# Five raw weight buffers and five ring slots instead of three and six, with a new deal of the low parts, in a two-block transformer kernel

## The chip, the cores and the metric

The kernel runs on one core of one Trainium2 chip. The metric is the device time of one execution in microseconds (us); smaller is better. All activations stay on the chip; the weights, 364 pieces of 512 KB, stream from HBM while TensorE (PE) works.

## The reference, cut to what matters

Batch 1, 256 tokens (T), model width 1024. The first block has two hybrid layers, the second one layer:

```python
for layer in range(2):                                  # hybrid_layer
    p = split_columns(rmsnorm(x, norm_g) @ w_in)        # 19 groups of columns
    qk = silu(causal_dwconv(concat(p.ml_q, p.ml_k)))    # 4 taps
    y_ml  = norm(mlstm(...) * sigmoid(ml_o)) * silu(ml_z)
    y_gla = norm(gla(...)) * silu(gla_r)
    y_dsa = attention(top-64 keys by index score, + rel_bias[bucket(j - i)]) * silu(dsa_z)
    x = x + concat(y_ml, y_gla, y_dsa) @ w_out
h = x + 0.5 * swiglu(norm(x), ffn1)                     # 1024 -> 2816 -> 1024
n = norm(h)
attn  = causal attention, 8 heads of 64
zg    = gelu(...);  gm = zg_u * (W_s @ layernorm(zg_v) + b_s)   # spatial gating
gates = sigmoid(n @ w_gate + b_gate)
h = h + (gates_a * (attn @ wa) + gates_b * (gm @ wb)) @ w_out
h = h + 0.5 * swiglu(norm(h), ffn2)
out = norm(h)
```

Everything is float32.

## The kernel before

**Tiling.** Activations lie transposed: 128 channels on the partitions, 256 tokens along the free dimension. A weight piece ("slot") is 128 x 1024, eight tiles of 128 x 128. Each layer uses 90 slots (74 for `w_in`, 16 for `w_out`), each FFN 66, the mixer 20 + 16 + 8 + 8. A product is done in three matmuls per weight tile: weight and activation are both split into a part rounded to float32r ("high") and the rest ("low"), and high x high, low x high and high x low are summed in PSUM. So a slot is 24 matmuls of 256 columns (or 12 of 512). `xs` holds both parts of the normed input, `ys` those of the input to an output projection.

**The weight pipeline.** SyncE (SP) loads slot g into `raw[g % 3]` as soon as `lo[g % 3]` says that the low part of slot g-3 was made. ScalarE (ACT) copies it, rounded, to `ring[g % 6]` high (`split`, line 392) after PE has used slot g-6 (`slots_used`). VectorE (DVE, line 854, one instruction of 1024 columns) makes the low part of every third slot, GpSimd (POOL, line 291, two halves) that of the others. PE waits on `lo` before it uses a slot. On ACT, DVE and POOL `split(p)` stands in a written-out order between the other work of position p and converts slot p + RING.

**The stages.** In front of each layer, FFN and mixer, PE begins on the input before the norm's factor is known (`first_two`, `early`, line 409), because the factor can be multiplied to the results afterwards (`early_result`, line 892). Squares of `x` are summed (lines 398, 871, 1496), ACT forms the root (`factor`, lines 373 to 380, with a table load), DVE refines it (883 to 887), the normed input is written to PSUM (`normed`, 898) and split again into `xs` (`norm` on ACT, line 424, `norm_lo` on DVE, line 910), and the later products read that. `norm` stands behind the first few `split`s in ACT's order. In a layer PE's first small matmuls after that (line 1641, index logits) wait for DVE's and ACT's gate work (`gate_softplus` 497, `gate_scan` 965 to 974) and `early_result(5)`. From slot 12 to 26 come the small products of gated linear attention (eight levels, lines 1067 to 1097, 1693), from 26 the convolution (`convolve`, line 1154, whose PSUM bank PE waits for), then gates (491, 1207 to 1211), then `w_out` (`sum_slot`, line 1557).

**At the start** one matmul forms the relative bias rows (4 x 384), ACT copies them (line 434) and issues one DMA (line 438) that writes each row 128 times to DRAM (`bias_rows`, 4 x 128 x 384).

**FFN.** Per tile f of 128 hidden channels three slots: gate, up (line 1509), and the down slot of tile f-2 (1557). DVE does lines 1288, 1293, 1298, 1302 and the low part 916, ACT the tanh (683) and the high part (688).

**Mixer.** In `spatial` PE does line 1933 after the layer norm (DVE line 1405), DVE adds the bias and multiplies (1413, 1414). ACT's `branch_hi` (773) and DVE's `branch_lo` (1418) split the eight branch inputs, four of them at the last gate slot; the branch products (line 1509, 12 matmuls each) wait for four low parts at a time.

## Time and profile before

| what | value |
|---|---|
| median of 3 runs | 1270.58 us (1267.05 to 1275.13) |
| the profiled execution | 1263.89 us, span of its instructions 1262.0 us |
| mean granted TensorE clock | 0.974 of 2.4 GHz |
| busy: PE, DVE, ACT, POOL | 1173.5, 823.0, 655.4, 698.7 us |
| weights and other data moved | 199.66 MB, mean 158 GB/s |

The profiled execution lies 1.89 us above its span and 6.69 us below the median. A group's row gives its busy time, the mean of one instruction, and the idle time of the engine ahead of it with what ended it. A PE that waits inside a run of matmuls can be shown busy, since ends of matmuls are modelled; counts of matmuls in a stretch tell more than its busy time.

### The profile page before, as it was taken

The page shows a single profiled execution, that of the slowest core. Times are in us where ns is not written, and L with a number is a line of the kernel's source. Part 1 is how long each engine was busy: PE and PEld are TensorE (multiplying, and loading weights), DVE is VectorE, ACT ScalarE, POOL GpSimd, SP SyncE. Part 2 cuts the span into 40 slices and gives each one's busy share as a digit, 9 for nine tenths or more (in the row PEclk, how much of TensorE's full clock was granted, in tenths as well). Part 3 has the DMA queues.
Part 4 walks back from the last instruction along what each step waited for, and adds up shares of the span by engine and source line. Part 5 has one row for each costly group of instructions (what it writes and reads, how often), then busy time and mean ns, then how long its engine had stood idle before and what let it go on. Part 6 is the DMA issues. An engine that isn't in the chain of part 4 may idle for free.

```text
span 1262.0 us, 25299 instructions
## 1 busy us (share of the span) xinstructions
PE 1173.5 (93%) x9214; PEld 1111.7 (88%) x9214; DVE 823.0 (65%) x1301; ACT 655.4 (52%) x1020; POOL 698.7 (55%) x530
## 2 busy tenths in 40 slices
PE   5499998999998989999999999999899889999996
PEld 4488798899997969989999999998878889999996
DVE  4366979486667598866676645555656756655664
ACT  3464485346456637644655544444657435544442
POOL 2243547555655355664566576667565555666662
PEclk9698999999998999999999999999999989999999
DMA  6343334544554433354456455555453445566561
GB/s 208 94 137 122 125 115 150 168 157 163 177 163 149 135 123 105 134 185 143 162 180 204 157 197 189 198 193 185 149 174 127 141 144 175 167 200 200 187 196 50
DMA packets 57715, 199.66 MB, mean 158 GB/s; under 512 B 6388, under 2 KB 9492, under 8 KB 57620
## 3 DMA queue, kind: packets, MB, share of 16 engines
q1 hardware_dynamic: 53856, 193.90, 46.6%
q10 hardware_dynamic: 3764, 4.47, 1.5%
q8 instruction: 62, 1.02, 0.3%
q14 instruction: 33, 0.27, 0.1%
HBM read 196.52 MB, written 1.84 MB: 157 GB/s over the span
## 4 chain that ended last, share of the span: by engine, by line
PE 29%; POOL 28%; issue 23%; DVE 11%; DMA 5%; ACT 3%; POOLq 0%; DVEq 0%; ACTq 0%; SPq 0%
POOL ring L291 26%; PE ps L1509 18%; PE ps L1557 6%; DMA raw<-in_w 5%; PE ps L1547 2%; DVE ring L854 2%; ACT ring L392 1%; DVE gs L1067 1%; PE ps L1660 1%; POOL dec L305 1%; DVE gat L1097 0%; ACT xs L424 0%; DVE xs L1418 0%; DVE xs L864 0%; POOL dec L306 0%
## 5 line engine op out<-in xcount | busy, mean ns | idle before, releaser
L291 POOL TENSOR_TENSOR ring<-raw,ring 128x512 fp32r<-128x512 f32 x484 | 666.8, 1401 | 510.2 <-ACT ring L392 508.8
L1509 PE MATMUL ps<-xs,ring 128*128 128x256 f32 x5424 | 666.7, 283 | 32.9 <-DVE mq L892 15.9
L1509 PEld LDWEIGHTS ps<-xs,ring 128*128 128x128 f32 x5424 | 647.4, 192 | 45.2 <-issue 17.5
L392 ACT ACTIVATE ring<-raw 128x1024 fp32r<-128x1024 f32 x364 | 382.5, 1055 | 251.6 <-DMA raw<-in_w 197.2
L854 DVE TENSOR_TENSOR ring<-raw,ring 128x1024 fp32r<-128x1024 f32 x122 | 179.0, 1467 | 156.6 <-ACT ring L392 154.6
L1557 PE MATMUL ps<-ys,ring 128*128 128x256 f32 x2016 | 240.2, 278 | 4.1 <-DVE ys L916 2.9
L1557 PEld LDWEIGHTS ps<-ys,ring 128*128 128x128 f32 x2016 | 235.8, 188 | 4.8 <-issue 3.5
L1547 PE MATMUL ps<-ring,xs 128*128 128x512 f32 x480 | 120.6, 404 | 6.4 <-DVE xs L910 3.2
L1547 PEld LDWEIGHTS ps<-ring,xs 128*128 128x128 f32 x480 | 88.9, 190 | 28.0 <-issue 9.1
L1154 DVE SCALAR_TENSOR_TENSOR ca<-ps,par,ca 128x253 f32<-128x253 f32 (+2 forms) x96 | 45.1, 477 | 11.4 <-ACT ca L476 10.0
L916 DVE TENSOR_TENSOR ys<-ca,ys 128x256 fp32r<-128x256 f32 x44 | 42.2, 960 | 13.8 <-ACT ys L688 13.8
L683 ACT ACTIVATE ex<-ex 128x256 f32<-128x256 f32 x44 | 18.1, 415 | 61.2 <-DVE ex L1288 61.2
L491 ACT ACTIVATE ex<-ps 128x256 f32<-128x256 f32 x48 | 18.3, 382 | 53.6 <-PE ps L1509 53.5
L916 DVE TENSOR_TENSOR ys<-y,ys 128x256 fp32r<-128x256 f32 x32 | 30.0, 938 | 23.2 <-ACT ys L619 23.1
L1519 PEld LDWEIGHTS ps<-xs,ring 128*128 128x128 f32 x240 | 31.0, 204 | 10.8 <-issue 8.7
L1519 PE MATMUL ps<-xs,ring 128*128 128x256 f32 x240 | 31.9, 297 | 8.8 <-ACT xs L409 5.7
L688 ACT ACTIVATE ys<-ca 128x256 fp32r<-128x256 f32 x44 | 18.2, 413 | 39.4 <-DVE ca L1302 39.3
L1293 DVE SCALAR_TENSOR_TENSOR ca<-ps,rms 128x256 f32<-128x256 f32 x44 | 18.3, 417 | 29.0 <-PE ps L1509 29.0
L1302 DVE SCALAR_TENSOR_TENSOR ca<-ex,ca 128x256 f32<-128x256 f32 x44 | 32.4, 737 | 1.5
L1298 DVE TENSOR_TENSOR ca<-ca,ex 128x256 f32<-128x256 f32 x44 | 30.8, 700 | 1.4
L476 ACT ACTIVATE ca<-ps,par 128x256 f32<-128x256 f32 x32 | 17.8, 557 | 25.4 <-DVE mq L1169 13.8
L538 ACT ACTIVATE gs<-gs 128x256 f32<-128x256 f32 x16 | 6.8, 423 | 45.7 <-DVE gs L1067 45.7
(256 smaller groups left out, 1053.9 us busy)
## 6 DMA issues: line engine op xcount, KB each, us to landing
raw<-in_w SPq DMA_DIRECT2D x364, 512.0 KB, 3.5
y<-bias_rows ACTq DMA_DIRECT2D x6, 256.0 KB, 3.2
x<-in_x SPq DMA_DIRECT2D x4, 256.0 KB, 7.1
out_y<-y SPq DMA_DIRECT2D x4, 256.0 KB, 2.2
const<-in_const SPq DMA_DIRECT2D x1, 896.0 KB, 10.7
bias_rows<-lg ACTq DMA_DIRECT2D x1, 768.0 KB
par<-in_par ACTq DMA_DIRECT2D x3, 181.0 KB, 2.4
dec<-in_wT ACTq DMA_DIRECT2D x1, 512.0 KB, 4.7
```

The costliest lines, as they stand in the source:

```text
L291: last = pool.tensor_tensor(ring[:, g % RING, 1, half], raw[:, g % RAW, half], ring[:, g % RING, 0, half].bitcast(F32), ALU.subtract)
L392: act.activation(ring[:, g % RING, 0, :], raw[:, g % RAW, :], ACT.Copy).then_inc(S["hi"], 1)
L491: ins = act.activation(ex[:, m % 4, :], src[:, 0:T], ACT.Tanh, scale=0.5)
L854: tt(ring[:, g % RING, 1, :], raw[:, g % RAW, :], ring[:, g % RING, 0, :].bitcast(F32), ALU.subtract).then_inc(lo[g % RAW], 1)
L916: tt(ys[:, at, 1, :], src, ys[:, at, 0, :].bitcast(F32), ALU.subtract).then_inc(S["y_lo"], 1)
L1154: ins = stt(dst[:, late:T], bank[:, 0:T - late], w[:, j:j + 1], dst[:, late:T], ALU.mult, ALU.add)
L1298: step(tt(ca[:, f % 2, :], ca[:, f % 2, :], ex[:, 2 + f % 2, :], ALU.mult))
L1302: stt(ca[:, f % 2, :], ex[:, f % 2, :], 1.0, ca[:, f % 2, :], ALU.add, ALU.mult)\
L1509: last = mm(ps[bank][:, half * T:(half + 1) * T], ring[:, slot % RING, wp, (at + k) * P:(at + k + 1) * P], rhs(k, xp), start=(i == 0), sto ...
L1519: return mm(ps[bank][:, 0:T], ring[:, slot % RING, wp, k * P:(k + 1) * P], rhs(k, xp), start=start, stop=stop)
L1547: last = mm(ps[banks[tt]][:, :], xs[:, 2 * q + k, xp, tt * P:(tt + 1) * P], ring[:, slot % RING, wp, k * 512:(k + 1) * 512], start=(q == 0 ...
L1557: ins = mm(ps[4 + n // 2][:, n % 2 * T:(n % 2 + 1) * T], ring[:, slot % RING, wp, n * P:(n + 1) * P], ys[:, at, xp, :], start=(first and n ...
```

## The change

Five edits, made together:

1. `RAW` 3 to 5 and `RING` 6 to 5. A raw buffer and a ring slot now have the same index, and each load waits for the low part of the slot five before.
2. Who makes a low part is told by the stage (`on_vector`): in a layer positions 3 and 6, then every fourth up to 42, then every third; in an FFN every second, in the mixer every third. POOL makes the others.
3. The relative bias is formed on all 128 partitions by four matmuls (one head each), copied by four activations of 128 x 384, and stored by one DMA whose source is those 128 partitions.
4. The spatial product stays in PSUM, its jobs on PE and DVE come one slot later, and the first branch products wait for each part by itself instead of four.
5. The FFN loops are unrolled on all engines, SP's loops too. Besides: at the start the loads of `x` and slot 1 are interleaved and `par` is asked for after `rb` and `hot`; in a layer `row_results` and `gate_softplus` come earlier in ACT's order, and two explicit table loads are dropped.

```diff
-RAW = 3
-RING = 6
+RAW = 5
+RING = 5
+def on_vector(p):
+
+    if p < 0:
+        return p in (-RING, -RING + 3)
+    if p < LAYER_SLOTS:
+        if p < EARLY + 2:
+            return p in (3, 6)
+        return p % 4 == 2 if p < 42 else p % 3 == 0
+    if FFN1_AT <= p < MIX_AT or p >= FFN2_AT:
+        f = p - FFN1_AT if p < MIX_AT else p - FFN2_AT
+        return f % 2 == 1 and f < FFN_SLOTS - 4
+    return p % 3 == 0
...
-            sp.dma_start(raw[:, 0, :], d["w"][0]).then_inc(slot_in[0], 16)
-            for c in range(N_UPDATES):
+            fetch(0, 0)
+            for c in range(2):
                 sp.dma_start(x[:, 2 * c:2 * c + 2, :], d["x"][:, 2 * c:2 * c + 2, :]).then_inc(x_in[c], 16)
...
+            fetch(1, 1)
+            for c in range(2, N_UPDATES):
+                sp.dma_start(x[:, 2 * c:2 * c + 2, :], d["x"][:, 2 * c:2 * c + 2, :]).then_inc(x_in[c], 16)
+            for g in range(2, RAW):
+                fetch(g, g)
...
+            for g in range(RAW, TOTAL_SLOTS):
+                sp.wait_ge(lo[g % RAW], g // RAW)
+                fetch(g, stored_at(g))
...
-            act.wait_ge(S["bias_ps"], 1)
-            act.activation(bias_row, ps[5][0:4, 0:HOT], ACT.Copy).then_inc(S["bias_sb"], 1)
+            for h in range(4):
+                act.wait_ge(S["bias_ps"], h + 1)
+                act.activation(relu4[:, h, :], ps[4 + h][:, 0:HOT], ACT.Copy).then_inc(S["bias_sb"], 1)
             split(-RING + 3)
             squares(0)
-            act.wait_ge(S["bias_sb"], 1)
-            act.dma_start(bias_rows.ap(), bias_row.rearrange("h (o n) -> h o n", o=1).broadcast_to((4, P, HOT)))\
-                .then_inc(S["bias_out"], 16)
+            act.wait_ge(S["bias_sb"], 4)
+            act.dma_start(bias_rows.ap().rearrange("h p n -> p h n"), relu4).then_inc(S["bias_out"], 16)
...
                 def gate_softplus():
-                    log_and_exp()
...
                 split(1, it, LAYER_SLOTS)
+                row_results()
                 split(2, it, LAYER_SLOTS)
-                row_results()
                 split(3, it, LAYER_SLOTS)
                 norm(it, gains, V_G, it * LAYER_SLOTS + EARLY)
+                gate_softplus()
                 split(4, it, LAYER_SLOTS)
                 split(5, it, LAYER_SLOTS)
-                gate_softplus()
...
                 g = p + RING
-                if g % RAW == 0:
+                if on_vector(p):
                     dve.wait_ge(S["hi"], reg * per + (g + 1))
...
-                dst = ca[:, pr % 2, :]
+                dst = ps[4 + pr][:, T:2 * T]
                 step(tt(dst.rearrange("p (c i) -> p c i", c=2), src, b, ALU.add))
-                stt(y[:, pr, :], y[:, pr, :], 0.5, dst, ALU.mult, ALU.mult).then_inc(S["sg_done"], 1)
+                stt(dst, y[:, pr, :], 0.5, dst, ALU.mult, ALU.mult).then_inc(S["sg_done"], 1)
...
-                     29: [(spatial, 0), (spatial, 1)], 31: [(spatial, 2), (spatial, 3)]}
+                     30: [(spatial, 0), (spatial, 1)], 32: [(spatial, 2), (spatial, 3)]}
...
-            mm(ps[5][0:4, 0:HOT], rb[:, :], hot, start=True, stop=True).then_inc(S["bias_ps"], 1)
+            for h in range(4):
+                mm(ps[4 + h][:, 0:HOT], rb[:, h:h + 1].broadcast_to((32, P)), hot,
+                   start=True, stop=True).then_inc(S["bias_ps"], 1)
...
-            jobs2[29] = [(spatial, 0), (spatial, 1)]
-            jobs2[31] = [(spatial, 2), (spatial, 3)]
+            jobs2[30] = [(spatial, 0), (spatial, 1)]
+            jobs2[32] = [(spatial, 2), (spatial, 3)]
...
-                    if n == 0:
-                        pe.wait_ge(S["b_lo"], 4 * g + 4)
-                    last = tile_product(n % 4, g, slot, lambda k, part: branch(4 * g + k, part), range(4), at=4 * g)
+                    last = tile_product(n % 4, g, slot, lambda k, part: branch(4 * g + k, part), range(4), at=4 * g,
+                                        ready=(lambda k, part: pe.wait_ge(
+                                            S["b_lo" if part else "b_hi"], 4 * g + k + 1)) if n == 0 else None)
```

## Rows read from the trace of the kernel before

**Rows 1.** The waits, all engines and then PE's: who waited for whom, us, times, longest.
```profile
ACT ring L392 <- DMA raw<-in_w: 197.2, 127, 15.9
...
PE ps L1693 <- DVE gat L1095: 4.7, 2, 2.3
```

**Rows 2.** FFN1 and FFN2: us, busy (xmatmuls), other engines' busy, PEclk, DMA share, GB/s.
```profile
713.00:880.00 167.00, 166.81 (x1421) 166.25 (x1421) 88.96 (x120) 77.98 (x101) 115.11 (x81) 1.00 0.57 192
...
1082.00:1246.00 164.00, 164.00 (x1450) 164.00 (x1449) 99.41 (x124) 75.31 (x100) 102.59 (x76) 1.00 0.56 180
```

**Rows 3.** The timeline of the first 71 us: start, duration, instruction, idle before.
```profile
16.24 1.24 ACTq L438 DMA_DIRECT2D bias_rows<-lg  x1
...
21.79 1.13 PE L1496 MATMUL ps<-y,const 128*128 128x256 f32 x4 [0.72 <-DVE y L871]
...
36.25 1.06 ACT L392 ACTIVATE ring<-raw 128x1024 fp32r<-128x1024 f32 x1 [15.93 <-DMA raw<-in_w]
...
39.85 1.28 ACT L373 ACT_TABLE_LOAD   x1
...
43.83 0.42 DVE L892 SCALAR_TENSOR_TENSOR mq<-ps,rms 104x256 f32<-104x256 f32 x1
...
53.71 1.06 ACT L392 ACTIVATE ring<-raw 128x1024 fp32r<-128x1024 f32 x1 [10.79 <-DMA raw<-in_w]
...
70.39 0.49 PE L1641 MATMUL ps<-ik,mq 64*128 64x128 f32 x4 [1.66 <-ACTq L457]
```

**Rows 4.** DMA from 14 to 58 us: busy share in tenths, GB/s, ACT's queue.
```profile
DMA  6067485267527722222222225932222267682100
GB/s 252 37 164 306 63 222 164 22 68 239 138 22 156 250 24 22 22 52 69 70 79 77 68 71 91 293 68 22 22 25 25 22 149 264 192 354 115 52 7 0
...
q10 hardware_dynamic: 516, 0.79, 15.0%
```

**Rows 5.** The timeline of the same place in layer 1.
```profile
378.56 0.42 DVE L892 SCALAR_TENSOR_TENSOR mq<-ps,rms 104x256 f32<-104x256 f32 x1
...
387.15 1.06 ACT L392 ACTIVATE ring<-raw 128x1024 fp32r<-128x1024 f32 x1 [3.13 <-DMA raw<-in_w]
...
388.72 11.04 PE L1509 MATMUL ps<-xs,ring 128*128 128x256 f32 x72 [3.71 <-ACT xs L424]
...
395.23 1.10 DVE L965 SCALAR_TENSOR_TENSOR gat<-gat 4x256 f32<-4x256 f32 x1 [1.24 <-ACT gat L498]
...
400.98 0.49 PE L1641 MATMUL ps<-ik,mq 64*128 64x128 f32 x4 [1.22 <-ACTq L457]
```

**Rows 6.** Busy time of a short stretch; PEclk is the third number from the end.
```profile
388.00:400.00 12.00, 11.04 (x72) 10.87 (x72) 9.68 (x15) 7.14 (x14) 6.96 (x4) 0.76 0.36 125
```

**Rows 7.** The timeline of FFN1 at 789 us, and of FFN2 at 1104.
```profile
789.85 5.82 PE L1509 MATMUL ps<-xs,ring 128*128 128x256 f32 x48
...
1104.42 5.60 PE L1509 MATMUL ps<-xs,ring 128*128 128x256 f32 x48
```

**Rows 8.** The timeline of the mixer, from its entry to its branch products.
```profile
883.46 5.89 PE L1519 MATMUL ps<-xs,ring 128*128 128x256 f32 x48 [2.99 <-ACT xs L409]
...
904.46 1.06 ACT L392 ACTIVATE ring<-raw 128x1024 fp32r<-128x1024 f32 x1 [5.39 <-DMA raw<-in_w]
...
909.59 3.23 DVE L910 SCALAR_TENSOR_TENSOR xs<-ps,gains,xs 128x256 fp32r<-128x256 f32 x8 [1.81 <-ACT xs L424]
910.61 2.99 PE L1547 MATMUL ps<-ring,xs 128*128 128x512 f32 x12 [3.22 <-DVE xs L910]
...
993.92 1.44 PE L1933 MATMUL ps<-dec,gv 128*64 128x128 f32 x16 [3.23 <-DVE gv L1405]
...
1013.54 5.55 DVE L1418 TENSOR_TENSOR xs<-y,xs 128x256 fp32r<-128x256 f32 x4 [1.80 <-ACT xs L773]
...
1019.14 2.93 PE L1509 MATMUL ps<-xs,ring 128*128 128x256 f32 x12 [3.32 <-DVE xs L1418]
```

**Rows 9.** DVE's groups in FFN1, 720 to 880 us: busy, mean ns, idle before.
```profile
L854 DVE TENSOR_TENSOR ring<-raw,ring 128x1024 fp32r<-128x1024 f32 x19 | 29.5, 1550 | 58.6 <-ACT ring L392 58.6
```

More of the change, by code:

```diff
@@ L45 @@
 IN_SLOTS, OUT_SLOTS = 74, 16
+EARLY, M_EARLY = 6, 8
 LAYER_SLOTS = IN_SLOTS + OUT_SLOTS
@@ L286, in split @@
                 g = p + RING
-                if g % RAW:
+                if not on_vector(p):
                     pool.wait_ge(S["hi"], reg * per + (g + 1))
@@ L333, in ffn @@
             def ffn(at):
-                for p in range(4):
-                    split(at + p)
-                loops = (FFN_TILES - 2) // 4 - (1 if at == FFN2_AT else 0)
-                with pool.Fori(0, loops) as i:
-                    for p in range(12):
-                        split(at + 4 + p, i, 12)
-                for p in range(at + 4 + 12 * loops, at + FFN_SLOTS):
+                for p in range(at, at + FFN_SLOTS):
                     if p + RING < TOTAL_SLOTS:
@@ L712, in ffn @@
                 split(at + 3)
-                loops = (FFN_TILES - 2) // 4 - (1 if last else 0)
-                with act.Fori(0, loops) as i:
-                    four(i, 2)
-                if last:
-                    four(0, 2 + 4 * loops)
-                else:
+                for f in range(2, FFN_TILES):
+                    tile(f)
+                if not last:
                     act.wait_ge(S["par2_in"], 16)
@@ L772, in branch_hi @@
                     act.wait_ge(S["xs_free"], (LAYERS + 1) * (KT - 1) + k - 3)
-                act.activation(branch(k, 0), y[:, (k + 4) % 8, :], ACT.Copy).then_inc(S["b_hi"], 1)
+                act.activation(branch(k, 0), branch_in(k), ACT.Copy).then_inc(S["b_hi"], 1)
             def layer_root():
@@ L1248, in _ @@
                     normed(it, c)
-                split(0, it, LAYER_SLOTS)
                 for r in range(2, 4):
@@ L1253, in _ @@
                 gate_abs()
-                split(3, it, LAYER_SLOTS)
+                for p in range(EARLY):
+                    split(p, it, LAYER_SLOTS)
                 early_result(4)
@@ L1284, in ffn, with gate, up @@
             def ffn(at, n, h_done, y_done, last):
[L1286 to L1287 removed]
+                def gate(f, slot):
+                    dve.wait_ge(S["slots_used"], slot + 1)
                     stt(ex[:, 2 + f % 2, :], ps[2 * (f % 2)][:, 0:T], -0.5, rms[:, 0:T], ALU.mult, ALU.mult)\
                         .then_inc(S["ffn_t"], 1)
[L1291 to L1292 removed]
+                def up(f, slot):
+                    dve.wait_ge(S["slots_used"], slot + 1)
@@ L1312, in four @@
-                def four(i, f0):
-                    step.restart()
-                    for f in range(f0, f0 + 4):
-                        p = at + 4 + 3 * (f - 2)
-                        gate(f, p, i)
-                        next_split(p, i)
-                        up(f, p + 1, i)
-                        up_gate(f, i)
-                        product(f, i)
-                        next_split(p + 1, i)
-                        product_lo(f, i)
-                        next_split(p + 2, i)
+                        split(p)
@@ L1325, in ffn, with tile @@
+                def tile(f):
+                    p = at + 4 + 3 * (f - 2)
+                    gate(f, p)
+                    next_split(p)
+                    up(f, p + 1)
+                    up_gate(f)
+                    product(f)
+                    next_split(p + 1)
+                    product_lo(f)
+                    next_split(p + 2)
                 factor(n)
@@ L1334, in ffn @@
                     split(p)
-                loops = (FFN_TILES - 2) // 4 - (1 if last else 0)
-                with dve.Fori(0, loops) as i:
-                    four(i, 2)
-                if last:
-                    four(0, 2 + 4 * loops)
+                for f in range(2, FFN_TILES):
+                    tile(f)
                 update_x(n, at + FFN_SLOTS, 0.25)
@@ L1440, in _ @@
                 normed(LAYERS, c)
-            split(MIX_AT)
-            split(MIX_AT + 3)
+            for p in range(MIX_AT, MIX_AT + 5):
+                split(p)
             for r in range(4, 7):
@@ L1445, in _ @@
             norm_lo(LAYERS, gains2, U_MIX)
-            split(MIX_AT + 6)
+            for p in range(MIX_AT + 5, MIX_AT + M_EARLY):
+                split(p)
             early_result(7)
```

126 lines of the change are left out of this document (50 added, 76 removed).

## The prediction

> **What bounds the kernel now.** I read the busy times first (PE is the fullest, 1173.5 of 1262.0 us in the table), then counted matmuls per stretch, since a PE that waits can look busy. 364 slots of 24 matmuls (value slots: 12 of double width) are 8736 units. In FFN2 PE does 1450 matmuls in 164 us, 0.1131 us each, so one slot costs 2.71 us and the weights alone 988 us [rows 2]. The other 274 us are the smaller products, half-rate clock, and waits. So any stretch in which PE runs at the FFN2 rate cannot gain, and the question is where it does not.
>
> Then the waits. ACT waited 197.2 us in 127 waits for weights, the longest 15.9 us [rows 1]: a raw buffer is reloaded only after its low part is made. Most of that costs PE nothing; what matters is where ACT's next job is on PE's path. The timeline shows three kinds of places. At the start, ACT stands 15.93 us and later 10.79 us at a load, and the norm's factor and the second split of the input are queued behind those [rows 3]. At the norm of layer 1 it stands 3.13 us, at that of the mixer 5.39 us [rows 5, 8]. In FFN1 PE is slower than in FFN2: 1421 matmuls in 167 us, 0.1175 us each, at the same granted clock of 1.00 [rows 2]; 48 matmuls take 5.82 us instead of 5.60 [rows 7]. I call the two the slow and the fast step of PE. I found the slow step to begin after short waits of PE in several places, and it stays for a long time after supply has recovered; this is an observation of order, not a shown cause.
>
> **The change part by part**, against the profiled execution (1263.89 us).
>
> *Start.* The DMA issued at 16.24 us has 512 packets of 1.5 KB. For long stretches after it the DMA engines together are 0.2 to 0.3 busy and move 22 to 79 GB/s, ahead of it and after it up to 354 [rows 4]: that is a few of the 16 engines, full, while each weight load needs its share of these few too. Its queue has 516 packets in 15.0% of 16 engines over 44 us, 105.6 engine-us, 0.205 us a packet [rows 4]. The new source has 128 partitions, so I expect all 16 engines with 32 packets each: 6.6 us at this price, and no load waits longer than that. The Trainium skill, page "DMA: Bandwidth & Descriptors", section "Why a DMA increments its semaphore by 16 and not by 1", says that the slowest dimension of both access patterns sets the number of engines, 4 before and 16 after; the trace agrees by its share of about 4/16.
>
> After the change slots 0 to 4 are asked for at once. Their 2.5 MB, x and the constants are about what is moved before 20 us now, so slot 5 should land by about 23 us. PE is through the first two results about when it starts on the squares, 21.79 us [rows 3]; the four copies of 128 x 384 cost ACT some 1.5 us more there. ACT then does one split (1.06), and from its table load (39.85) to the first scaled result (43.83) are 3.98 us [rows 3]: 23 + 1.06 + 3.98 = 28. From that instruction to PE's line 1641 layer 1 takes 400.98 - 378.56 = 22.4 us [rows 5], and 6 less after the next item: 28 + 16.4 = 44.4, against 70.39 [rows 3]. That is 26; for the copies and for `par`, asked for later, I take 1 off: **25**. Bounds: 6 if loads still stall as before, 29.
>
> *Norm of layer 1.* The load wait of 3.13 us ahead of slot 99 goes, since with five buffers its buffer is free five slots earlier. `norm` starts about 3.5 us earlier, so PE's 3.71 us of idle time goes [rows 5]. The granted clock there was 0.76 on average, so part of it was at 1.2 GHz: 72 matmuls took 11.04 us, against 8.14 at the fast step [rows 6]. But the path then runs over DVE's gate chain, which waited 1.24 us for the table load and activations [rows 5]; PE gets ready earlier than it and waits there longer than now (1.22 us). Earlier start 3.5, no table load 1.3, earlier `gate_softplus` 1: **6**. Bounds 2 and 8. The splits of positions 4 and 5 now stand behind `gate_softplus`; they hide behind the three products of 8 us.
>
> *FFN1 and FFN2.* If FFN1's 20 tiles run at FFN2's rate, 1421 x (0.1175 - 0.1131) = 6.3 us. In both FFNs DVE will make a low part that PE needs soon right behind its first two tiles, today only in FFN1; in FFN2 I take off most of one such part, 1.3 of 1.55 us [rows 9]: **5**. Bounds 0 and 8. Unrolling itself I cost at nothing: PE shows no gap at a loop's end in FFN2 (1450 matmuls in 164 us are three slots each 8.14 us, all of it).
>
> *Mixer.* Entry: PE idles 2.99 us [rows 8], with a low part on DVE just ahead of the update of x; POOL makes it after the change, so the mean price of one, 1.5 [rows 9]. Norm: the 5.39 us load wait of ACT goes, PE's 3.22 us of idle time too: 3. Spatial, first pair: PE waits 3.23 us for the layer norm, one slot later (2.7 us) it waits 0.5: 3, and 1 for the clock. Branch inputs: DVE's four low parts took 5.55 us, 1.39 each, PE waited 3.32, and the next 12 matmuls took 2.93 us against 1.4 [rows 8]. From PSUM and released one by one nothing is left of that wait; the twelve matmuls lost 1.6 us to the slower rate behind it, and I count two batches like that: 3.3 + 3.2 = 6.5. Sum **15**. Bounds 7 and 18.
>
> The Trainium skill, page "SBUF — State Buffer", section "Who interferes with whom", says that a DVE instruction with two SBUF inputs and a GpSimd instruction that reads SBUF block each other in full, one with a single SBUF input does not. Rows agree: from PSUM eight low parts took 3.23 us, 0.40 each [rows 8], beside POOL. The rule speaks for the branch edit and against more low parts on DVE in the FFNs.
>
> *Inside the layers.* DVE has two low parts less between positions 15 and 25 of a layer (2 instead of 4), where PE waited 4.7 us in two waits for it [rows 1], and 1.5 us is what one costs on average [rows 9]; POOL has two more. I take 2 us for both layers together (bounds -5 and 8: POOL also makes the level keys that PE waits for). The `w_out` products wait less for an ACT that stands at loads, and the slow step behind such waits goes in some places: 5 (bounds 0 and 10). Sum **7**.
>
> *One ring slot less.* ACT may start a slot when PE is done with the fifth before, not the sixth, 2.7 us later at most. What hides it is the lead of the low part over PE; PE's waits name a late low part at only a few places of FFN1. So 0; without that cover a late place costs up to 2.7 us once. Bounds 0 and -4.
>
> Total: 25 + 6 + 5 + 15 + 7 = **58**, and 1263.9 - 58 = 1206 on the scale of the profiled execution. The median lies 6.7 us above it, and a few of three runs of the changed kernel should lie as much above theirs: I shift by 3 and predict **1209**. The lower bounds of all items give a gain of 6 + 2 + 0 + 7 - 5 - 4 = 6, the upper ones 73; not all fall together.
>
> **The rivals.**
> 1. *Only the start gains.* The other waits turn into waits for DVE's chains (gates, layer norm), which are as long as before: 1263.9 - 25 - 8 + 3 = 1234. For it: PE's waits ahead of lines 1641 and 1933 are ends of DVE chains. Against it: in four of the places a load wait of ACT or a clock loss is seen in the row itself. Chance 0.12.
> 2. *The change doesn't do what it says at the start*: the new DMA of bias rows, now on every engine, or the 1 MB more of early loads delays slot 5 as long as today. Gain there 6: 1209 + 19 = 1228. For it: the packets are of the same small size. Against: 32 on an engine instead of 128. Chance 0.06.
> 3. *Slower: DVE becomes the bound of the FFNs.* It decides when DVE's time per tile passes PE's 8.14 us. Now it is 99.41 us for 20.1 tiles, 4.9 us [rows 2]. Half a low part more is 0.8 us; and it waits for ACT ahead of each, 58.6 us in 19 [rows 9], 3.1 us, now 1.5 times a tile: 4.9 + 0.8 + 4.6 = 10.3 us in the worst case. Then 40 tiles lose 2.16 us each, 86 us, against 53 gained elsewhere and with the shift of 3: 1264 + 86 - 53 + 3 = 1300. Against it: most of that waiting is for work that would otherwise be idle time, and POOL, less busy, blocks DVE less. Chance 0.03. The rule of the Trainium skill's page "SBUF — State Buffer" named above would lengthen the low parts themselves in this case.
> 4. *More than forecast*: the slow step vanishes everywhere and the layers' DVE waits too: 1192. Chance 0.10.
>
> **How the numbers follow.** The forecast, 1209, within 1198 to 1220: 0.65. With rivals 1, 2 and 4 it makes 0.93, with the slow one 0.96; the remaining 0.04 are gains that come to nothing in a way not listed. The range 1190 to 1236 holds the forecast, rivals 1, 2 and 4, and leaves out the slower case and gains of nothing. Within 1% of 1270.58 (1258 to 1283), about what a measurement of this kernel can tell from no change: 0.04. Slower by over 1%: 0.03. Faster: 0.93.
>
> **What the changed profile would show.** ACT has no wait for a load over 5 us in the first 60 us, and line 1641 runs at 42 to 48 us. PE's wait ahead of the norm's products in layer 1 is under 1 us. FFN1 and FFN2 have the same matmuls per us. PE's waits for lines 1405 and 1418 are under 1 us together, and the clock is not halved behind them. ACT's sum of waits for loads falls from 197.2 us to under 60. The prediction is wrong if new waits of PE for low parts (POOL or DVE) add up to more than 10 us, if the slow step spreads, or if DVE's gate chain swallows the early norm.

## The result and the profile after

The kernel before: median 1269.15 us (1267.05 to 1275.13, 4 runs). The changed kernel: **1233.17 us** (1217.06 to 1237.33, 4 runs). Ratio 0.9667, 95% interval 0.9564 to 0.9769: faster. Forecast were 1209 us, range 1190 to 1236. Measured again in a later experiment the same kernel had 1228.46 us (1224.01 to 1231.32, 6 runs), ratio 0.972 (0.9677 to 0.9763). So some 36 us were gained of the 61 forecast. The execution profiled after the change is the slowest of its four (1237.33 us, span 1235.3), 1.7% over the fastest, so it counts as slow and the ratio leaves it out. The experiment e6_same gives a second trace, of a shorter execution of the same kernel (1224.01 us, span 1221.9); what is said of the layers and the FFNs is given for both.

First the waits of the changed kernel (who waited for whom, us, times, longest), of ACT and then of PE:

```profile
ACT ring L398 <- DMA raw<-in_w: 12.1, 5, 3.8
...
PE ps L1506 <- DVE ca L1155: 8.4, 2, 4.2
PE ps L1584 <- DMA emr<-in_hot: 6.2, 1, 6.2
PE ps L1692 <- DVE gat L1096: 5.6, 2, 2.9
PE ps L1692 <- DVE gat L1098: 3.8, 5, 1.0
...
PE ps L1506 <- DVE ring L855: 1.6, 1, 1.6
PE ps L1923 <- DVE gv L1401: 1.4, 1, 1.4
```

ACT's 197.2 us of waiting for weights [rows 1] are 12.1. PE's list is headed by something that had no place in the forecast: 8.4 us for the convolution's taps. Before, the same wait had 3.9 us, but a second one for the taps, 120 matmuls later in each layer, had 3.2 us more and is now gone:

```profile
PE ps L1509 <- DVE ca L1154: 3.9, 2, 1.9
...
PE ps L1547 <- DVE ca L1154: 3.2, 2, 1.8
```

Then, after the change, the start, layer 1 and the end of the mixer, from the timeline:

```profile
8.70 1.06 ACT L398 ACTIVATE ring<-raw 128x1024 fp32r<-128x1024 f32 x1 [2.87 <-DMA par<-in_par]
...
16.37 0.39 ACTq L445 DMA_DIRECT2D bias_rows<-lg  x1
...
25.96 0.42 DVE L893 SCALAR_TENSOR_TENSOR mq<-ps,rms 104x256 f32<-104x256 f32 x1
...
43.49 0.49 PE L1640 MATMUL ps<-ik,mq 64*128 64x128 f32 x4 [0.94 <-ACTq L463]
...
352.85 1.02 PE L1493 MATMUL ps<-y,const 128*128 128x256 f32 x4
...
353.52 19.42 PE L1506 MATMUL ps<-xs,ring 128*128 128x256 f32 x168
...
374.22 0.49 PE L1640 MATMUL ps<-ik,mq 64*128 64x128 f32 x4 [1.28 <-ACTq L463]
...
971.63 1.15 PE L1923 MATMUL ps<-dec,gv 128*64 128x128 f32 x16 [1.41 <-DVE gv L1401]
...
987.72 1.52 PE L1506 MATMUL ps<-ys,ring 128*128 128x256 f32 x12
```

PE's line 1640 (1641 before) runs at 43.49 us, at 70.39 before [rows 3]. In layer 1 PE does 168 products without a gap where it stood 3.71 us [rows 5], and in the mixer the branch products start with no wait and twelve take 1.52 us, where 2.93 us stood behind a wait of 3.32 [rows 8].

The starts of some matmuls cut the kernel into stretches, the same ones in every trace: the first of the index logits in each layer (70.39 and 400.98 before), and the sums of squares at the head of each block (21.79, 373.08, 697.61, 889.93 and 1073.52 before; 21.63, 352.85, 680.09, 868.37 and 1039.88 after). The start ends at the first index logits. The lengths, in us:

| kernel | start | layer 0 | norm 1 | layer 1 | FFN1, to the mixer's norm | mixer | FFN2 and end |
|---|---|---|---|---|---|---|---|
| before | 70.4 | 302.7 | 27.9 | 296.6 | 192.3 | 183.6 | 188.5 |
| after | 43.5 | 309.4 | 21.4 | 305.9 | 188.3 | 171.5 | 195.4 |
| e6_same (after again) | 42.9 | 307.6 | 21.4 | 301.9 | 182.0 | 170.9 | 195.2 |
| e1_bias | 51.1 | 304.7 | 26.2 | 302.5 | 193.7 | 180.9 | 188.5 |
| e2_unroll | 69.1 | 299.9 | 26.2 | 302.8 | 199.7 | 181.7 | 188.4 |
| e7_row | 50.7 | 308.3 | 21.4 | 303.8 | 188.5 | 171.0 | 195.2 |
| e11_ring | 47.6 | 303.3 | 22.3 | 303.0 | 188.4 | 172.9 | 195.2 |
| e8_spatial | 43.2 | 308.2 | 21.4 | 298.7 | 188.5 | 179.3 | 189.0 |
| e3_deal | 43.5 | 300.3 | 21.4 | 298.2 | 188.3 | 171.5 | 195.5 |
| e12_early | 43.2 | 305.3 | 21.4 | 300.1 | 182.7 | 168.6 | 189.6 |

Start, norm and mixer gained 26.9 + 6.5 + 12.1. Both layers lost, 6.7 and 9.3 (4.9 and 5.3 in e6_same), and FFN2 lost 6.9 (6.8). The experiments ask what made the gains, and why the layers and the FFNs lost.

For the layers a first answer is in the granted clock, the third number from the end: layers 0 and 1 before, then layers 0 and 1 after (columns as in rows 2):

```profile
70.39:373.08 302.69, 292.65 (x2200) 270.73 (x2201) 219.74 (x362) 167.71 (x272) 160.96 (x125) 0.97 0.45 148
400.98:697.61 296.63, 285.58 (x2200) 263.91 (x2201) 219.21 (x362) 167.96 (x272) 160.92 (x125) 0.99 0.47 155
```

```profile
43.49:352.85 309.36, 298.26 (x2201) 276.28 (x2202) 225.00 (x360) 167.83 (x272) 176.72 (x135) 0.95 0.48 147
374.22:680.09 305.87, 294.38 (x2201) 272.92 (x2201) 225.88 (x360) 166.78 (x271) 173.75 (x133) 0.97 0.49 151
```

In these traces the clock has two levels, 2.4 and 1.2 GHz. It stood at the lower one for 20.5 us of the two layers before, for 51.2 us after and for 47.8 us in e6_same. PE's idle times over 0.15 us there hardly differ in sum: 23.1, 24.0 and 22.5 us. What the lower level costs is an estimate: at the norm of layer 1, where the mean was 0.76 over 12 us, so 5.8 us at 1.2 GHz, 72 matmuls took 2.9 us more than at the fast step [rows 6]. At half a microsecond for each, 31 us more are up to 15 of the 16 us that the layers lost. The first 300 of a layer's 2200 matmuls show the clock almost alone. Over all 14 traces, whatever the kernel, they took 40.0 to 40.2 us with 3.4 us at 1.2 GHz, 41.7 to 41.9 with 6.8, 43.2 to 43.4 with 10.2, and 44.7 to 45.5 with 13.7. The kernel before had 10.2 and 3.4 us there, the changed one 13.7 twice, and 10.2 twice in e6_same. So 7.0 of the 16 us, and 3.4 of e6_same's 10, lie in a part in which one program differs between two executions; what sets the clock there is open.

Here are the FFNs of the changed kernel (us, busy and matmuls of PE, its weight loads, DVE, ACT, POOL, PEclk, DMA share, GB/s):

```profile
694.00:869.00 175.00, 174.13 (x1475) 173.70 (x1474) 106.85 (x144) 81.86 (x115) 96.33 (x65) 1.00 0.59 188
1041.00:1206.00 165.00, 164.93 (x1401) 164.76 (x1400) 99.69 (x136) 74.27 (x102) 90.34 (x59) 1.00 0.58 182
```

165 us for 1401 matmuls are 0.1178 us each, against 0.1131 in FFN2 before [rows 2], with the granted clock at 1.00 both times. FFN2 has moved from the fast step to the slow one, and FFN1 is at the slow one, though nothing starves it any more. Between the starts of successive 256-column matmuls lie 113 ns or 118 ns, and hardly anything between, for long stretches.

### The profile page after: what moved, and what is told of

Same layout as the page of the kernel before. It is cut to its first block, busy times and chain, and to the rows that moved or that the text cites. A ratio compares the mean times of both kernels' runs of the same rounds, so it can differ in the third digit from the quotient of the medians.

```text
span 1235.3 us, 23603 instructions
## 1 busy us (share of the span) xinstructions
PE 1186.9 (96%) x9220; PEld 1125.1 (91%) x9220; DVE 840.3 (68%) x1312; ACT 644.2 (52%) x1019; POOL 687.4 (56%) x508
## 4 chain that ended last, share of the span: by engine, by line
PE 75%; DVE 16%; issue 4%; ACT 4%; DMA 1%; POOL 0%; ACTq 0%; DVEq 0%
PE ps L1506 42%; PE ps L1554 16%; PE ps L1544 7%; DVE ring L855 2%; DVE gs L1068 1%; PE ps L1692 1%; PE ps L1659 1%; PE ps L1783 1%; DVE rms L845 1%; DVE y L1196 1%; ACT ring L398 1%; DVE var L844 1%; DVE xs L865 1%; DVE y L1143 1%; DVE xs L911 1%
## 5 line engine op out<-in xcount | busy, mean ns | idle before, releaser
L303 POOL TENSOR_TENSOR ring<-raw,ring 128x512 fp32r<-128x512 f32 x462 | 656.9, 1446 | 498.0 <-ACT ring L398 496.6
L398 ACT ACTIVATE ring<-raw 128x1024 fp32r<-128x1024 f32 x364 | 377.4, 1050 | 110.0 <-PE ps L1554 47.1
L855 DVE TENSOR_TENSOR ring<-raw,ring 128x1024 fp32r<-128x1024 f32 x133 | 186.6, 1404 | 137.7 <-ACT ring L398 136.9
L1554 PE MATMUL ps<-ys,ring 128*128 128x256 f32 x2016 | 244.0, 281 | 2.6 <-DVE ys L917 2.2
L1554 PEld LDWEIGHTS ps<-ys,ring 128*128 128x128 f32 x2016 | 239.5, 189 | 3.4 <-issue 3.4
L917 DVE TENSOR_TENSOR ys<-y,ys 128x256 fp32r<-128x256 f32 x32 | 32.8, 1036 | 13.4 <-ACT ys L623 13.3
L1692 PEld LDWEIGHTS ps<-qke 64*128 64x128 f32 x240 | 15.7, 196 | 15.0 <-issue 14.7
```

The costliest lines, as they stand in the source:

```text
L303: last = pool.tensor_tensor(ring[:, g % RING, 1, half], raw[:, g % RAW, half], ring[:, g % RING, 0, half].bitcast(F32), ALU.subtract)
L398: act.activation(ring[:, g % RING, 0, :], raw[:, g % RAW, :], ACT.Copy).then_inc(S["hi"], 1)
L855: tt(ring[:, g % RING, 1, :], raw[:, g % RAW, :], ring[:, g % RING, 0, :].bitcast(F32), ALU.subtract).then_inc(lo[g % RAW], 1)
L917: tt(ys[:, at, 1, :], src, ys[:, at, 0, :].bitcast(F32), ALU.subtract).then_inc(S["y_lo"], 1)
L1554: ins = mm(ps[4 + n // 2][:, n % 2 * T:(n % 2 + 1) * T], ring[:, slot % RING, wp, n * P:(n + 1) * P], ys[:, at, xp, :], start=(first and n ...
L1692: last = mm(second(ps[6 + e][:, (2 * tt + pr) * P:(2 * tt + pr + 1) * P]), kk[rows, keys], second(qq[rows, queries]), start=True, stop=True)
```

## The experiments

**What the bias edit is worth alone (e1_bias), and what the rest is worth without it (e7_row).**

```diff
 e1_bias: before.py
-            mm(ps[5][0:4, 0:HOT], rb[:, :], hot, ...)
+            for h in range(4):
+                mm(ps[4 + h][:, 0:HOT], rb[:, h:h + 1].broadcast_to((32, P)), hot, ...)
 (with the four copies, the transfer and the order of ACT's first transfers as in the change)
 e7_row: after.py with the same lines turned back, the order of ACT's transfers left as changed
```

> The kernel before with the bias edit alone: the bias through 128 rows, and ACT's three first transfers in the changed order. Theory A (the start's gain is the bias transfer's alone, and layer 0 behind it runs as before): the first product of squares of layer 0 moves from 70.39 us to about 44, so the time falls by 25 to 27 us, ratio 0.979 to 0.981. Theory B (with three raw buffers the weights behind the start are late, and a part of it is given back before layer 1): the same place at about 44, but only 15 to 20 us at the end, ratio 0.984 to 0.988.

Measured: 1247.97 us (1243.13 to 1252.75), ratio 0.9862 (0.9807 to 0.9916). The size is that of theory B, the place is not: the index logits start at 51.10 us, not at 44, so what is missing is missing inside the start.

> The changed kernel with the bias back on four rows and its transfer broadcast from these (the order of ACT's three first transfers stays as changed). Theory A (the start's gain is the bias transfer's): the first product of squares of layer 0 moves from 43.49 us back to 68 to 71, and the time rises by 22 to 27 us against the changed kernel, to about 1257. Theory B (with five raw buffers the weights behind the start are in place earlier, and part of the start's gain comes from them; the bias alone gave 18 us): rise of 15 to 20 us, to about 1250.

Measured: 1238.50 us (1236.21 to 1240.65), ratio 0.9792 (0.9738 to 0.9846), 10.0 us over e6_same in the same comparison. Both theories had the loss too large. The start of e7_row:

```profile
15.60 1.24 ACTq L444 DMA_DIRECT2D bias_rows<-lg  x1
...
35.52 1.06 ACT L398 ACTIVATE ring<-raw 128x1024 fp32r<-128x1024 f32 x1 [6.87 <-DMA raw<-in_w]
38.01 1.06 ACT L398 ACTIVATE ring<-raw 128x1024 fp32r<-128x1024 f32 x1 [1.43 <-DMA raw<-in_w]
...
50.74 0.49 PE L1638 MATMUL ps<-ik,mq 64*128 64x128 f32 x4 [1.37 <-ACTq L463]
```

The narrow transfer is the same as before, but ACT stands 6.87 + 1.43 us at loads where it stood 15.93 and then 10.79 [rows 3]: more weights are in place when it begins. The bias edit alone, or all the other edits without it, brings the index logits from 70.4 to about 51, 19 us; both bring 26.9. They are two cures of the same waits, and their gains overlap by 12. No run has the five buffers alone, so how much of the second 19 us is theirs is not shown; with the bias edit in place they are worth 4 us at the start (47.63 in e11_ring, 43.49 in the changed kernel). The Trainium skill, page "DMA: Bandwidth & Descriptors", section "Why a DMA increments its semaphore by 16 and not by 1", lets 128 rows spread over 16 engines. The wide transfer landed 6.1 us after its issue in the changed kernel, 4.8 in e1_bias.

**Three raw buffers in the changed kernel (e11_ring).**

```diff
-RAW = 5
-RING = 5
+RAW = 3
+RING = 6
```

> The changed kernel with three raw buffers and six ring slots, everything else as changed (the deal of low parts by stage too). The bias edit alone gave 18 us where all edits gave 27 at the same place of the start, and the changed kernel with the bias back on four rows kept 19 of them. Theory A (five raw buffers are worth about as much as the bias edit at the start, and the two overlap; behind the start the transfers are again what ACT waits for): 12 to 20 us slower than the changed kernel (8 to 9 at the start, the rest in the norm of layer 1 and short waits in the FFNs), about 1243 to 1248. Theory B (the deal of the low parts and the order of the transfers did it, not the count of buffers): within 4 us of the changed kernel.

Measured: 1233.44 us (1229.22 to 1237.77), ratio 0.9734 (0.9685 to 0.9783), 5 us over e6_same at nearly the same median of before; the intervals overlap. Its ACT:

```profile
ACT ring L398 <- DMA raw<-in_w: 141.4, 107, 6.0
```

ACT's waits for loads are 141 us again, 129 more than in the changed kernel, and against e6_same the trace shows 4.7 us more at the start, 0.9 in the norm and 2 in the mixer. Theory A asked for more than twice the 5 us measured, theory B is nearer. The sum of waits that made the case for the buffers in the first place is almost all slack.

**The FFNs unrolled and nothing else (e2_unroll).** The FFN functions of all five engines as in the change, in the kernel before.

> The kernel before with the FFNs (and the weight transfers' queue) unrolled, and nothing else: three raw buffers, six ring slots, every third low part on DVE. Theory A (the loops cost nothing that ends a wait of PE; what PE's rate in an FFN hangs on is the step of a matmul, 113 or 118 ns, and which of them it falls into): within 1% of before, ratio 0.994 to 1.004, and each FFN lies wholly at one of the two steps, with a change of step only where PE had a wait of its own. Theory B (the loops' heads cost PE time in each of their rounds): faster by 5 us or more, ratio under 0.996, in both FFNs alike.

Measured: 1268.38 us (1261.71 to 1274.63, 12 runs), ratio 1.0021 (0.9991 to 1.005). No gain: theory B is out. FFN1 took 7.4 us longer than before, with nine short waits of PE for POOL's low parts (3.9 us), FFN2 the same 188.4.

**The mixer's edits turned back (e8_spatial).**

```diff
-            return y[:, 4 + k, :] if k < 4 else ps[k][:, T:2 * T]
+            return y[:, (k + 4) % 8, :]
...
-                dst = ps[4 + pr][:, T:2 * T]
+                dst = ca[:, pr % 2, :]
...
-            jobs2[30] = ...; jobs2[32] = ...
+            jobs2[29] = ...; jobs2[31] = ...
-                    ... ready=(lambda k, part: pe.wait_ge(S["b_lo" if part else "b_hi"], 4 * g + k + 1)) ...
+                    if n == 0:
+                        pe.wait_ge(S["b_lo"], 4 * g + 4)
```

> The changed kernel with the mixer's spatial product back in SBUF, its jobs back at slots 29 and 31, and the first output product waiting for all four low parts of the branches. Theory A (the two waits of PE there, 3.22 and 3.32 us before, the clock at half behind the second, and the wait ahead of the spatial products come back; between slots 270 and 288 of the sequence the changed kernel gained 10.3 us on the one before): 8 to 11 us slower than the changed kernel. Theory B (the gain there is that of the five raw buffers and the deal of the low parts): under 3 us slower.

Measured: 1233.91 us (1230.18 to 1239.2), ratio 0.9771 (0.9728 to 0.9814), 5.4 over e6_same, with intervals that overlap. In the trace the mixer takes 179.3 us, and 170.9 to 171.5 in the seven others that leave the mixer as changed: 8 us, theory A by the place if not by the median. PE's two waits are back:

```profile
PE ps L1923 <- DVE gv L1401: 4.2, 1, 4.2
...
PE ps L1506 <- DVE xs L1414: 3.3, 1, 3.3
```

**The deal of low parts in the layers (e3_deal).** The convolution's wait is where I looked first. The changed kernel, then the one before, then e3_deal, each at the gated norm of layer 0:

```profile
166.25 2.20 DVE L844 TENSOR_TENSOR var<-var,rms 128x1024 f32<-128x1024 f32 x1
...
169.89 3.99 DVE L1143 SCALAR_TENSOR_TENSOR y<-y,gains,rms 128x256 f32<-128x256 f32 x4
170.14 2.87 POOL L303 TENSOR_TENSOR ring<-raw,ring 128x512 fp32r<-128x512 f32 x2
...
174.00 0.48 DVE L1155 SCALAR_TENSOR_TENSOR ca<-ps,par,ca 128x253 f32<-128x253 f32 x1
...
175.78 1.43 PE L1506 MATMUL ps<-xs,ring 128*128 128x256 f32 x5 [4.18 <-DVE ca L1155]
```

```profile
194.14 1.75 DVE L1142 SCALAR_TENSOR_TENSOR y<-y,gains,rms 128x256 f32<-128x256 f32 x4
...
197.80 1.42 PE L1509 MATMUL ps<-xs,ring 128*128 128x256 f32 x10 [1.95 <-DVE ca L1154]
```

```profile
163.80 1.75 DVE L1143 SCALAR_TENSOR_TENSOR y<-y,gains,rms 128x256 f32<-128x256 f32 x4
...
167.46 2.77 PE L1506 MATMUL ps<-xs,ring 128*128 128x256 f32 x22 [1.95 <-DVE ca L1155]
```

```diff
-        return p % 4 == 2 if p < 42 else p % 3 == 0
+        return p % 3 == 0
```

> The changed kernel, with every third low part of a layer (from its ninth slot on) on DVE, where it has every fourth up to slot 41. Theory A (low parts that POOL makes beside DVE's operations with two inputs in SBUF slow these down: the four of the gated norm took 3.99 us in the changed kernel, with a low part of POOL from 170.14 to 173.01, and 1.75 us before, with none): the wait of PE ahead of the convolution's slot falls from 4.18 us to about 2, in both layers, the waits in the level stage by 1 to 3 us a layer, and the time by 6 to 10 us against the changed kernel. Theory B (DVE needs the room: it was near its limit in the levels, and a low part of 1.23 us more in its queue costs as much as it saves): no change within 2 us, waits only moved.

Measured: 1225.08 us (1220.63 to 1227.4), ratio 0.9687 (0.9649 to 0.9724). Against e6_same (0.972) the medians show 3 us and do not separate the two; the traces do. The slot that position 33 of a layer converts has its low part on POOL by the changed rule and on DVE by the other one. On POOL it falls into the four operations of the norm, and the first tap of the convolution and PE wait behind them: 3.99 us for four instead of 1.75, 4.18 us of PE instead of 1.95. By the Trainium skill, page "SBUF — State Buffer", section "Who interferes with whom", a VectorE instruction with two inputs in SBUF contends with a GpSimd instruction that reads SBUF. The trace agrees: in all six traces with the changed deal (after, e6, e4, e7, e8, e11) these four operations had 1074 ns in the median, in the eight others 472 to 474 ns. The first wait in the levels fell as well, from 2.9 and 2.7 us to 2.3 in both layers.

The longer wait is not all loss and not the whole cost. The second wait for the taps, which the changed kernel does not have, comes back in e3_deal:

```profile
PE ps L1544 <- DVE ca L1155: 2.7, 2, 2.3
```

And behind the longer wait the clock falls for longer. Here are 14.2 us behind it in layer 0, first of the changed kernel, then of e3_deal: 97 matmuls at a mean of 0.78, and 120 at 1.00.

```profile
175.78:190.00 14.22, 14.21 (x97) 14.22 (x98) 13.66 (x24) 11.38 (x18) 9.25 (x9) 0.78 0.39 129
```

```profile
167.46:181.70 14.24, 14.09 (x120) 13.89 (x120) 13.68 (x24) 10.70 (x18) 12.82 (x12) 1.00 0.55 160
```

Between the first wait and the 1100th matmul of the layer, PE had 6.8 us at 1.2 GHz in 11 of the 12 layers with the wait of 4.2 us, and 3.4 us or none in all 16 with the wait of 1.95.

Whole layers scatter too much for a price: 298.7 to 309.4 us in the six traces with the changed deal, 298.2 to 305.3 in the five with the other (e3, e5, e9, e10, e12). Counted by matmuls from the first index logits, two parts of a layer separate the deals. The 300th to the 500th, with the first level waits, took 36.2 to 36.6 us with the changed deal and 34.9 to 35.5 in the eight other traces. The 800th to the 1100th, with both waits for the taps, took 49.5 to 50.6 against 47.5 to 49.4. On average that is 1.4 + 1.8 us a layer over the five with the other deal, and as much in sum over the three kernels with the deal of before (before, e1_bias, e2_unroll). So the deal costs some 6 us in both layers, the lower end of theory A.

**The slow step: can it be broken from inside? (e4_fp32, e5_one, e9_turn, e10_turns).**

```diff
 e4_fp32: after.py, in each FFN (and e5_one: e3_deal with f == 3 alone)
                     here(slot)
+                    if f % 4 == 3:
+                        mm(ps[2 * (f % 2)][:, T:2 * T], ones, const[:, 0:T], start=True, stop=True)
 e9_turn: e3_deal with, at f == 3 of each FFN
+                        pe.transpose(ps[2 * (f % 2)][:, T:T + P], ones, ident)
 e10_turns: e9_turn, transpositions in the output slots and behind the last scores, and
+    if p == MIX_AT:
+        return False
```

> The changed kernel, with one more matmul ahead of every fourth tile of both FFNs: ones by 256 columns of the constants, in full fp32, into the idle half of the tile's bank (ten in all, about 0.43 us each, 4 us of added work; the output stays). Theory A (a short wait in the middle of a run of products puts PE into the 118 ns step, where it stays until another kind of matmul comes between; in the two traces every wait of 0.05 us or more inside a run of products at full clock was followed by 118 ns, and the sums of squares mostly by 113): the FFNs go back to 113 ns from the first added matmul on, about 6 us less in each FFN, and the time falls by some 8 us net against the changed kernel. Theory B (the step is drawn by something else, a place or a buffer, and the added matmuls only cost): 4 us slower than the changed kernel, steps as they were.

Measured: 1232.66 us (1229.43 to 1236.02), ratio 0.9744 (0.9705 to 0.9782). Neither: FFN1 entered its fourth tile at 118 ns and the five added matmuls were followed by 113, 118, 118, 118 and 113 ns; the same five in FFN2 by 113, 118, 118, 118 and 113. An added matmul changes the step, but both ways. And "every wait" brings 118 ns, as I had read from two traces, does not hold in the later ones.

> The changed kernel with the deal of e3_deal (every third low part of a layer on DVE) and one added matmul (ones by 256 columns of the constants, in full fp32) in each FFN, ahead of its fourth tile. In the run with an added matmul ahead of every fourth tile the one at this place was followed by 113 ns in both FFNs. Theory A (the step of a matmul is drawn where the run of products is broken, by a wait or another kind of matmul, and is then held; the draw depends on the place in the program): from that place on 113 ns in both FFNs, 6 to 6.5 us less in each, about 12 us less than e3_deal (1225.08 us), so about 1213, ratio 0.959. Theory B (the place does not decide; the draw is by chance): one FFN or none at 113 ns in the profiled run, and no or half of the gain in the median.

Measured: 1221.98 us (1217.12 to 1224.18), ratio 0.9666 (0.9623 to 0.9708). 113 ns in FFN1, 118 in FFN2: theory B. That the two FFNs of e4_fp32 agreed was chance.

> The changed kernel with the deal of e3_deal and one added transposition (ones, 128 by 128, into the idle half of the bank) in each FFN ahead of its fourth tile, in place of e5_one's matmul of 256 columns. Counted over the ten traces so far: where the last matmul ahead of a run of products was a transposition, the run had 113 ns each time (60 of 60); behind a wait in a run of products at 113 it had 118 ns in 73 of 185 cases; behind the added matmul of 256 columns in 7 of 12. Theory A (the kind of matmul ahead of the run decides the step): from the fourth tile on both FFNs at 113 ns, in every execution, about 1213 to 1217 us, with a spread under 8 us. Theory B (the step is chance, and the kinds only seem to decide it): the FFNs as often at 118 as in e3_deal and e5_one, 1220 to 1226 us.

Measured: 1225.17 us (1220.57 to 1231.53), ratio 0.9683 (0.9645 to 0.9722). FFN1 at 118, FFN2 at 113: theory A falls, a transposition does not bring the fast step.

> e9_turn with the mixer's first low part on POOL (PE waited 1.77 us for it on DVE), a transposition ahead of the fifth, ninth and thirteenth of a layer's output slots, and one behind each product of the layers' last scores (products behind that kind had 118 ns in 20 of 20 cases). Theory A: as e9_turn, 1.5 us less for the low part, 1.5 to 2 us less in each layer behind the scores and 0 to 2 in each layer's output slots, less about 0.12 us for each of the 14 added transpositions: 4 to 7 us under e9_turn. Theory B (chance): only the low part counts, 0 to 2 us under e9_turn.

Measured: 1225.67 us (1223.92 to 1227.22), ratio 0.9677 (0.9643 to 0.9711): theory B. The mixer took 168.7 us instead of 171.3, the low part's doing; FFN1 and FFN2 were both at 118.

**The same kernel again (e6_same).** No edit.

> The changed kernel itself once more, unchanged, beside the others of this call. Theory A (what made its four runs differ, from 1217.06 to 1237.33 us, is drawn anew in every execution: the granted clock and the step of the matmuls): again a median of 1228 to 1236 us with a spread of over 10 us, and FFNs that in the new trace can lie at another step than in the first. Theory B (the step belongs to the place in the program): both FFNs at 118 ns again, and only stretches in the layers differ.

Measured: 1228.46 us (1224.01 to 1231.32). Its FFNs:

```profile
688.00:855.00 167.00, 166.63 (x1469) 166.28 (x1467) 107.31 (x143) 80.40 (x114) 95.60 (x64) 1.00 0.63 196
1041.00:1206.00 165.00, 164.63 (x1398) 164.46 (x1397) 97.05 (x127) 70.79 (x97) 89.17 (x59) 1.00 0.56 173
```

FFN1 does 1469 matmuls in 167 us, 0.1137 each, where the same program took 0.1186 in the first trace; 6.3 us between 188.3 and 182.0. FFN2 is at 0.118 again. So the step is not written into the program: theory A.

**No wait where the FFN turned slow (e12_early).** In e3_deal both FFNs were entered at 113 ns and went to 118 behind a wait of 0.54 us ahead of the fourth tile, for a low part of POOL. It was late because ACT made that slot's high part behind the second tanh and two products.

```diff
                 gate_tanh(0)
+                split(at + 2)
                 gate_tanh(1)
                 product_hi(0)
                 product_hi(1)
-                split(at + 2)
                 split(at + 3)
+    if p == MIX_AT:
+        return False
```

> e3_deal with two more edits and no added matmul: the mixer's first low part on POOL (PE waited 1.77 us for it on DVE; in e10_turns the same edit took 1.9 us off at that place), and in each FFN ACT's high part of the third slot ahead of the second tanh and the two products, where it stood behind them. In e3_deal that high part began 6.0 us after its slot was free, its low part came 0.2 us late, PE waited 0.54 us ahead of the fourth tile of both FFNs, and both then ran at 118 ns to their ends, though both had been entered at 113. Theory A (the step of a matmul is drawn anew where a run of products is broken and held else; behind the sums of squares it was 113 ns in 40 of 50 cases, behind a wait in 112 of 185): without that wait an FFN keeps the step with which it is entered, mostly 113 ns: no change of step inside the FFNs of the profiled run, and 8 to 13 us under e3_deal (1225.08 us), about 1214. Theory B (the place of the fourth tile or what the other engines do there brings the slow step, wait or no wait): both FFNs change to 118 ns about there again, and the time falls by 2 to 4 us only, to about 1222.

Measured: **1214.68 us** (1211.35 to 1216.12), ratio 0.9558 (0.9519 to 0.9597), the fastest of all. FFN1 and FFN2 by windows, and from the timeline the head of FFN1's sum for its first tile:

```profile
684.00:848.00 164.00, 164.00 (x1449) 164.00 (x1449) 103.19 (x136) 76.24 (x107) 93.44 (x62) 1.00 0.62 200
1036.00:1195.00 159.00, 159.00 (x1405) 159.00 (x1404) 97.93 (x127) 70.64 (x97) 88.39 (x58) 1.00 0.57 182
```

```profile
683.12 3.01 PE L1556 MATMUL ps<-ys,ring 128*128 128x256 f32 x24 [0.67 <-DVE ring L857]
```

Both FFNs run at 0.1132. Against e3_deal the FFNs took 5.6 and 5.9 us less, the mixer 2.9. The size is theory A's, the way is not quite: the wait was not removed but replaced, by one of 0.7 to 0.8 us a slot earlier, for a low part of DVE, and behind that one both FFNs, which stood at 118, went to 113. So the gain of the edit rests on which kind of wait there is, or on luck in all its runs. Against luck speaks that the six lie within 5 us, where a draw in each FFN would set them up to 12 apart; the FFNs of only one of the six were traced. The last section has the counts.

## Why the prediction was right, and where its steps failed

The sum was 25 + 6 + 5 + 15 + 7 = 58 on the scale of the profiled execution. The measured 1233.17 us lie inside the range of 1190 to 1236, 3 us from its upper end, and outside the 1198 to 1220 that had 0.65. Most of the gain came where it was forecast, at the start, the norm and the mixer, 48.5 us in the profiled execution; the layers took back 15.9 of it, 10.2 in e6_same. One sum of the prediction is wrong too: the upper bounds of all items add up to 81, not 73, since the 8 for the low parts in the layers was left out. Item by item, by the table (after, and e6_same):

- *Start, 25*: 26.9 (27.5). The time of line 1641 was forecast at 44.4 and is 43.49. The mechanism is half of the story: the bias transfer alone gives 19, the other edits without it 19 as well. The 6 us that I kept as the item's lower bound, "if loads still stall as before", left out that the other edits work on the same waits. Rivals 1 (1234, only the start gains) and 2 (1228, the bias transfer doesn't help) are close to the measured time and wrong in their reasons: the norm and the mixer gained, and so did the start.
- *Norm of layer 1, 6*: 6.5. PE has no gap ahead of the norm's products. The deeper buffers need not be the cause: e11_ring, with three, has 22.3 for 21.4.
- *Mixer, 15*: 12.1 in the mixer (12.7), and FFN1's stretch holds the entry, where `first_two` no longer waits 2.99 us [rows 8]: 15.1. The spatial and branch edits are 8 of it by e8_spatial, where I had 4 + 6.5. The wait for line 1401 (1405 before) is 1.41 us, where I had said under 1, and the clock is not halved behind the branch inputs.
- *FFN1 and FFN2, 5*: **the first step that failed**, "if FFN1's 20 tiles run at FFN2's rate". I took the slow step for a trace of starvation that goes with it. ACT's starvation went (197.2 to 12.1 us), the step stayed: FFN1 gained about 1, FFN2 lost 6.9, a term of -6 in the profiled execution, about 0 in e6_same.
- *Inside the layers, 7*: **the second**. Measured are -15.9 in the profiled execution and -10.2 in e6_same. "2 us for both layers together", for low parts taken off DVE, has the wrong sign: the deal costs some 6. I had written that a DVE operation with two SBUF inputs and POOL block each other, and used it for the branch edit and for the FFNs; I did not walk along DVE's queue in the layers to see what each low part now on POOL would lie across. My bound of -5 was as far as I looked. And the granted clock, which I had priced at the norm and in the mixer, had no term in the layers at all: 20.5 us at 1.2 GHz before, 51.2 and 47.8 after. A part of that follows from the deal, behind the longer wait of the convolution; the rest differs from execution to execution, the kernel before was lucky in layer 1 (3.4 us in all, 13.7 in e1_bias and e2_unroll), and its cause stays open. The 5 us for the slow step did not come: matmuls at 118 ns in the layers went from 594 to 979, and to 634 in e6_same.
- *One ring slot less, 0*: nothing to the contrary; 5 raw buffers and 5 slots are 5 us better than 3 and 6 by the medians, with intervals that overlap.

In the order start, norm, layers, mixer with its entry, FFNs, the second trace has 27.5 + 6.5 - 10.2 + 15.6 + 0.6 = 40, which is 1262.0 - 1221.9 = 40.1. The median's gain is 36; the rest is what the profiled executions differ from their medians. Of rival 4 nothing came; rival 3's DVE, at 0.6 of the FFNs' time, never was the bound. Of the signs named in advance, the check on the start, the norm, ACT's sum (under 60) and the clock in the mixer held; that FFN1 and FFN2 have the same rate held in the profiled execution, at the wrong one; "the slow step spreads" was named as what would make it wrong, and did.

## What to carry to other kernels

A sum of waits is no price: ACT's waits for loads fell by 185 us, and taking 129 of them back cost some 5, hardly more than the medians can tell. When work is dealt out anew between VectorE and GpSimd, go along VectorE's queue and look at what each piece on the other engine now lies beside, for a piece of 2.9 us across four short operations made a wait of PE of 1.95 us into one of 4.18, in each layer. Price such a wait together with the next one on the same chain, which may shrink, and with the clock behind it. And two edits that cure the same wait have to be priced together, each also without the other.

## What the hardware showed that was not expected

PE has two steps at a granted clock of 1.00. In all 14 traces a run of 256-column products goes at 113 ns or at 118 ns a matmul and keeps its step to the next break, for 22 tiles and 180 us if nothing breaks it; a break is a wait, a rise of the clock or a matmul of another form. One whole FFN at the slow step costs 6.3 us (188.3 against 182.0 in two executions of one program). Two FFNs can so set two executions of one program 12 us apart. Whether the changed kernel, with fewer breaks, scatters more is not shown: 20 us between its first four runs, 7 between the six of e6_same, 8 to 18 between those of before.

What draws it is not settled. I counted the waits of 0.1 us or more inside such runs at full clock. Where the first matmul behind the wait is followed by the next after some 220 ns, the run went on at 113 ns in 48 of 58 cases; where after some 193 ns, in 26 of 77. The counts move by a few with how a run is delimited. The waits of e12_early in the FFNs are of the first kind, those of e3_deal of the second. Whether that sign is a cause, and what in the program decides it (the second kind often has two semaphores to wait for, but not always), was not tried. An added matmul or transposition is no remedy: it was followed by either step.
